# Two-block layer on one core: pass width in the plain projections, and the order of work in attention, pooling and key/value

## The chip, the cores and the metric

One core of a Trainium2 chip runs the kernel. The metric is the device time in microseconds, the median of the runs; before the change it is 3902.62 us (3 runs, 3899.95 to 3903.5). The profile is of one execution of its own, at 3903.91 us.

## The reference, cut to what matters

Two blocks follow each other on 256 tokens of width 2048, all in float32. The first: RMS norm, an input projection, a gated delta rule and a dilated attention, an output projection ("wout"), then a gated MLP with a 3-wide convolution ("up", 88 panels, and "down", 44 panels). The second also takes 256 context tokens. In short:

```
x  = x + mixed @ w_out                       # wout
up = conv3(norm(x) @ w_ffn_in); h = silu(gate) * val
x  = norm(x + h @ w_ffn_out)                 # down
h_lat, h_ctx = modulated norm of x and of ctx
q, k, v, gate = h @ w_in[...]                # q, gate: latent tokens; k, v: context too
y_na   = softmax(q k^T / 8 + bias) v         # 16 heads of 64, keys: a window and the context
y_pool = pooled mean - identity, mapped per group of channels, scaled
y_rw   = RWKV-7 scan over time, both ways, from k, v and a low-rank part ("lora")
merged = sum of gates * (branch @ w_branch);  x = x + gate * (merged @ w_out2)
```

## The kernel before, in words

A weight matrix comes in panels of 128 output channels by 2048 input channels (1 MB). SP loads panel p into one of two `ring` slots; ACT casts it to `w_hi` (fp32r, line 247), DVE subtracts it to get `w_lo` (line 253), and PE multiplies. `tick` does the cast or split of panel p+2 after panel p: the cast waits for `panel_used`, which PE raises when panel p is done, and SP loads p+2 when p is split. The activations are split in the same way. `project` (line 263) makes three passes of 256 columns for each of the 16 tiles of a panel: w_hi by x_hi, w_hi by x_lo, w_lo by x_hi, all summed in one 256-column range of PSUM bank 6 or 7. `project2` (line 278) does the same with 512 columns, latent and context tokens side by side. Matmuls of other kinds (sums over partitions, transposes, scores) have plain float32 operands.

The stages in order of time, and what they do around the change:

- wout (`add_*`, and `wout_tiles` for its first two panels). DVE adds the bank to `x` (line 1254), ACT makes `x_hi` and then casts, DVE makes `x_lo` and then splits.
- up (`up_*`). DVE multiplies the bank by the norm factor (line 1302), three convolution steps follow (1305, 1306, 1308), then the split of the panel after next, and a product or low half of the panel pair before (1290, 1294).
- down (`down_*`). 16 output tiles of 44 weight tiles each; the context tokens are normed beside it (`ctx_*`). At its end stands a chain: last bank to `x`, squares, a sum over channels on PE (line 1348), a root, a reciprocal (1471), and then for each of 16 tiles DVE (1476), ACT (1433, 1437), DVE (1479).
- attention (`na_*`). A hardware loop (Fori) of four passes on every engine, with two heads' pairs (u = 0, 1) in each. A pair has panels q, k, v, gate: q and gate by `project`, k and v by `project2`. Then come `v_rows` (1501), `scores` (1510), `turn_p` (1518) and `mix` (1527). For u = 0 these run between the panels of u = 1; for u = 1 they run after its last panel, at the end of the pass. Panel q of the first pair waits tile by tile for the chain above.
- A barrier of all engines; then GpSimd spills `x`, loads `PM` and `PWA`, and PE waits for them. Pooling (`pool_*`): a Fori loop of four, four panels each, then three small steps on PE that each wait for ACT (`u_turned`, `pooled`, `pool_y`; lines 1665 and 1672).
- A barrier; b_hi and b_lo of both branches in one piece each (2917, 2951); lora; key/value (`kv_*`): 8 pairs of panels k and v by `project2`. The sums and transposes of pair kt run after panel k of pair kt+1, those of the last pair at the end. GpSimd stores k and v to DRAM in six transfers a pair.
- A barrier; `rw_*`: 16 groups of the scan, between whose steps PE, ACT and DVE take quarters of 80 further panels (`fill_*`, each `F()` is a quarter: 4 tiles, or 12 passes of 256 columns). Five quarters precede the first group. What is left of the quarters runs at the end.
- tail, and wout2 (`last_*`), which is built like wout.

Of the kernel before, what the change touches and what calls it, by code (L numbers as in the profile page):

```python
# [152 lines left out]
def program(nc, a, out):  # L153
# [19 lines left out]
    x_hi = place("x_hi", 48, [P, KT, T], FR)  # L173
    x_lo = place("x_lo", 64, [P, KT, T], FR)
# [6 lines left out]
    def smalls(at_, n):  # L181
# [51 lines left out]
            ("na", 8, 4), ("pool", 4, 4), ("lora", 1, 1), ("kv", 2, 8), ("fill", 80, 1),  # L233
# [44 lines left out]
    def project2(pe, p, rhs, bank):  # L278
# [5 lines left out]
        for k in range(KT):  # L284
# [4 lines left out]
            last = nc.tensor.matmul(both, lo, xh, start=False, stop=k == KT - 1)  # L289
        last.then_inc(S("panel_used"), 1)  # L290
# [3 lines left out]

    bars = {}

    def barrier(eng):

        bars[id(eng)] = bars.get(id(eng), 0) + 1
        eng.drain().then_inc(S("phase_done"), 1)  # L300
        eng.wait_ge(S("phase_done"), 4 * bars[id(eng)])
# [744 lines left out]
    mx_hi = place("mx_hi", D0 + 48.5, [P, KT, T], FR)  # L1046
    mx_lo = place("mx_lo", D0 + 64.5, [P, KT, T], FR)
# [7 lines left out]
    def wout_tiles(pe, k0, k1):  # L1055
        for j in range(2):
# [5 lines left out]
            for k in range(k0, k1):  # L1062
                hi, lo = w_hi[:, s, k * P:(k + 1) * P], w_lo[:, s, k * P:(k + 1) * P]
                xh, xl = mx_hi[:, k, :], mx_lo[:, k, :]
                nc.tensor.matmul(pbank(p), hi, xh, start=k == 0, stop=False)
                nc.tensor.matmul(pbank(p), hi, xl, start=False, stop=False)
                last = nc.tensor.matmul(pbank(p), lo, xh, start=False, stop=k == KT - 1)
# [161 lines left out]
    def add_pe(pe):  # L1229
        for k in range(2, KT):  # L1230
            p = (first["wout"] + k, None, 0)
            project(pe, p, lambda t: (mx_hi[:, t, :], mx_lo[:, t, :]), pbank(p))
# [17 lines left out]
    def add_dve(dve, ch):  # L1250
        for k in range(KT):
            p = (first["wout"] + k, None, 0)
            dve.wait_ge(S("panel_used"), at(p, 3))
            nc.vector.tensor_tensor(x[:, k, :], pbank(p), x[:, k, :], ALU.add).then_inc(S("proj_read"), 1)
# [5 lines left out]
    h_hi = place("h_hi", W0 + 16, [P, FT, T], FR)  # L1260
    h_lo = place("h_lo", W0 + 60, [P, FT, T], FR)
    fraw = place("fraw", W0 + 104, [P, 2, 2, T + 2])
    fcv = place("fcv", W0 + 108.25, [P, 2, 2, T])

    def up_pe(pe):
        for k in range(2 * FT):
            p = (first["up"] + k, None, 0)
            project(pe, p, rhs_x, pbank(p))

    def up_act(act):  # L1270
# [15 lines left out]
    def up_dve(dve, ch):  # L1286
# [1810 lines left out]
```

## Time and profile before

| | |
|---|---|
| median of 3 runs | 3902.62 us |
| the profiled execution | 3903.91 us, of which the span is 3902.2 us |
| PE busy | 3585.3 us, 92% of the span |
| DVE busy | 2184.0 us, 56% |
| ACT busy | 1546.1 us, 40% |
| granted TensorE clock, mean | 0.960 of full |

The span goes from the first to the last instruction. Matmuls overlap in the record, so their durations add up to more than the time; the distance from start to start is what one of them costs.

### The profile page before, as it was taken

What the parts mean: (1) busy time and instruction counts of PE and PEld (TensorE: products, weight loads), DVE (VectorE), ACT (ScalarE), POOL (GpSimd) and SP (SyncE); (2) the same over time, 40 slices, a digit from 0 to 9 for tenths busy, and PEclk for the clock granted to TensorE, in tenths of its full rate; (3) what the DMA queues carried; (4) which work ended last, traced back from release to release, by engine and by line L of the source; (5) the groups of instructions that cost most, each with busy time, mean ns of one, the idle gap of its engine ahead of it and who ended that gap; (6) DMA issues with size and microseconds to landing.
All of it is one profiled execution on the core that took longest, in us unless ns stands there. A gap on an engine that the chain in (4) does not pass through costs nothing.

```text
span 3902.2 us, 85857 instructions
## 1 busy us (share of the span) xinstructions
PE 3585.3 (92%) x38442; PEld 3343.7 (86%) x38442; DVE 2184.0 (56%) x3247; ACT 1546.1 (40%) x2345; POOL 247.3 (6%) x306
## 2 busy tenths in 40 slices
PE   7999989999979999999978887899799999999978
PEld 7888989888879999999977776888688888888978
DVE  6666765556546777764443333345555655556554
ACT  4333333333334333334433333333444444444433
POOL 0021012000000000000000000001210111011000
PEclk9999999999989999999989998999899999999989
DMA  4534543565435555554532223324333333333354
GB/s 164 200 116 149 178 166 130 217 249 174 162 105 177 184 182 183 182 201 161 173 119 100 97 94 118 129 101 166 128 122 114 107 116 110 105 110 121 108 192 149
DMA packets 94390, 571.49 MB, mean 146 GB/s; under 512 B 12688, under 2 KB 20912, under 8 KB 32096
## 3 DMA queue, kind: packets, MB, share of 16 engines
q1 hardware_dynamic: 80496, 511.85, 37.1%
q0 software_dynamic: 13552, 54.49, 4.2%
q8 instruction: 287, 4.70, 0.5%
q14 instruction: 55, 0.45, 0.0%
HBM read 536.01 MB, written 30.28 MB: 145 GB/s over the span
## 4 chain that ended last, share of the span: by engine, by line
PE 76%; DVE 10%; ACT 6%; DMA 3%; issue 2%; POOL 1%; SPq 0%; DVEq 0%; ACTq 0%; POOLq 0%
PE banks L273 9%; PE banks L275 8%; PE banks L274 8%; PE banks L1911 3%; PE banks L966 3%; PE banks L1912 3%; PE banks L1913 3%; PE banks L967 2%; PE banks L968 2%; PE banks L1377 2%; PE banks L1379 2%; PE banks L1378 2%; PE banks L287 2%; PE banks L288 2%; PE banks L289 2%
## 5 line engine op out<-in xcount | busy, mean ns | idle before, releaser
L253 DVE TENSOR_TENSOR w_lo<-ring,w_hi 128x2048 fp32r<-128x2048 f32 x274 | 627.9, 2291 | 628.9 <-ACT w_hi L247 628.5
L247 ACT CAST w_hi<-ring 128x2048 fp32r<-128x2048 f32 x274 | 522.2, 1906 | 546.8 <-PE banks L275 388.8
L273 PE MATMUL banks<-x_hi,w_hi 128*128 128x256 f32 x1920 | 545.9, 284 | 6.8 <-DVE w_lo L253 6.5
L275 PE MATMUL banks<-x_hi,w_lo 128*128 128x256 f32 x1920 | 545.4, 284 | 0.0
L274 PE MATMUL banks<-x_lo,w_hi 128*128 128x256 f32 x1920 | 545.4, 284 | 0.0
L273 PEld LDWEIGHTS banks<-x_hi,w_hi 128*128 128x128 f32 x1920 | 370.6, 193 | 7.5 <-DVE w_lo L253 6.7
L274 PEld LDWEIGHTS banks<-x_lo,w_hi 128*128 128x128 f32 x1920 | 370.5, 193 | 0.0
L275 PEld LDWEIGHTS banks<-x_hi,w_lo 128*128 128x128 f32 x1920 | 370.5, 193 | 0.0
L1967 DVE TENSOR_TENSOR w_lo<-ring,w_hi 128x512 fp32r<-128x512 f32 x316 | 217.2, 688 | 248.4 <-ACT w_hi L1924 247.5
L966 PE MATMUL banks<-x_hi,w_hi 128*128 128x256 f32 x1152 | 349.0, 303 | 7.2 <-DVE w_lo L1033 7.2
L1911 PE MATMUL banks<-XK,w_hi 128*128 128x256 f32 x1024 | 320.3, 313 | 20.8 <-DVE w_lo L1967 20.8
L967 PE MATMUL banks<-x_lo,w_hi 128*128 128x256 f32 x1152 | 331.2, 287 | 0.0
L968 PE MATMUL banks<-x_hi,w_lo 128*128 128x256 f32 x1152 | 330.6, 287 | 0.0
L1912 PE MATMUL banks<-XK,w_hi 128*128 128x256 f32 x1024 | 293.5, 287 | 0.6 <-issue 0.6
L1913 PE MATMUL banks<-XK,w_lo 128*128 128x256 f32 x1024 | 292.8, 286 | 0.0
L1033 DVE TENSOR_TENSOR w_lo<-ring,w_hi 128x512 fp32r<-128x512 f32 x276 | 192.6, 714 | 128.2 <-ACT w_hi L1018 126.9
L966 PEld LDWEIGHTS banks<-x_hi,w_hi 128*128 128x128 f32 x1152 | 225.8, 196 | 25.3 <-issue 15.2
L1911 PEld LDWEIGHTS banks<-XK,w_hi 128*128 128x128 f32 x1024 | 199.1, 194 | 39.1 <-DVE w_lo L1967 23.1
L967 PEld LDWEIGHTS banks<-x_lo,w_hi 128*128 128x128 f32 x1152 | 226.5, 197 | 0.7 <-issue 0.5
L968 PEld LDWEIGHTS banks<-x_hi,w_lo 128*128 128x128 f32 x1152 | 225.7, 196 | 0.0
L287 PE MATMUL banks<-XK,w_hi 128*128 128x512 f32 x528 | 208.4, 395 | 1.4 <-DVEq L300 1.4
L1018 ACT CAST w_hi<-ring 128x512 fp32r<-128x512 f32 x276 | 164.3, 624 | 113.8 <-PE banks L968 65.4
(534 smaller groups left out, 8486.0 us busy)
## 6 DMA issues: line engine op xcount, KB each, us to landing
ring<-in_w_up SPq DMA_DIRECT2D x88, 1024.0 KB, 4.9
ring<-in_w_dil SPq DMA_DIRECT2D x72, 1024.0 KB, 4.9
mod_ring<-in_w_mod SPq DMA_DIRECT2D x48, 1024.0 KB, 7.6
ring<-in_w_logit SPq DMA_DIRECT2D x48, 1024.0 KB, 4.9
ring<-in_w_down SPq DMA_DIRECT2D x44, 1024.0 KB, 4.9
ring<-in_w_delta SPq DMA_DIRECT2D x32, 1024.0 KB, 4.9
ring<-in_w_out SPq DMA_DIRECT2D x32, 1024.0 KB, 4.8
ring<-in_w_na SPq DMA_DIRECT2D x32, 1024.0 KB, 4.8
```

The source lines that it names most:

```text
L247: nc.scalar.copy(w_hi[:, s, 0:w], ring[:, s, 0:w]).then_inc(S("panel_hi"), 4)
L253: nc.vector.tensor_tensor(w_lo[:, s, 0:w], ring[:, s, 0:w], w_hi[:, s, 0:w].bitcast(F32), ALU.subtract).then_inc(S("panel_split"), 1)
L273: nc.tensor.matmul(out_ap, hi, xh, start=k == 0, stop=False)
L274: nc.tensor.matmul(out_ap, hi, xl, start=False, stop=False)
L275: last = nc.tensor.matmul(out_ap, lo, xh, start=False, stop=k == tiles - 1)
L287: nc.tensor.matmul(both, hi, xh, start=k == 0, stop=False)
L966: nc.tensor.matmul(pbank(p), hi, xh, start=k == 0, stop=False)
L967: nc.tensor.matmul(pbank(p), hi, xl, start=False, stop=False)
L968: last = nc.tensor.matmul(pbank(p), lo, xh, start=False, stop=k == KT - 1)
L1911: nc.tensor.matmul(pbank(p), hi, xh, start=k == 0, stop=False)
L1912: nc.tensor.matmul(pbank(p), hi, xl, start=False, stop=False)
L1913: last = nc.tensor.matmul(pbank(p), lo, xh, start=False, stop=k == KT - 1)
```

## The change

Two edits. First, in wout, up, down and wout2 the passes are regrouped: the two activation halves lie side by side (`x_two`, `mx_two`, `h_two`, `m_two`), w_hi multiplies both in one pass of 512 columns into both halves of a PSUM bank, and w_lo multiplies the high half alone in a pass of 256 columns into the first half of the bank. The reader of the bank adds the two halves. Second, attention and pooling are written out without loops, the barriers from there to `rw_*` are gone, and the work of neighbouring stages overlaps:

- The panels of the first pair come as k, v, q, gate. `na_first` runs the context half of v and k (three passes of 256 columns a tile) before the latent half, whose tiles wait for the chain. `down_sum` of the last tile goes into it after four tiles. In the chain the gain moves from ACT to DVE, and ACT makes the high half in one activation instead of two; DVE runs two tiles behind with the low half (YB).
- Scores, turn_p and mix of each pair run between the panels of the next pair, those of the last pair between the first panels of pooling.
- Pooling's small steps run between the panels of the next group, the last group's within lora and key/value. `PM`, the spill and `PWA` are issued during attention; `PW` and its copy on GpSimd are gone. b_hi and b_lo are made in two pieces, in pooling and in the first pair of key/value.
- In key/value the sum over the squares of k runs inside panel v of the same pair; the last pair's transposes, mirrors and stores go into the start of `rw_*`, where eight quarters instead of five precede the first group. Waits on `kv_stored` stand ahead of the sigmoids (pairs 0 to 6) and of the first group (all 8), on ACT and DVE.

```
-    x_hi = place("x_hi", 48, [P, KT, T], FR)
-    x_lo = place("x_lo", 64, [P, KT, T], FR)
+    x_two = place("x_two", 48, [P, 2, KT, T], FR)
+    x_hi, x_lo = x_two[:, 0], x_two[:, 1]
...
+    def wide_tile(out_ap, hi, lo, both, first_, last_):
+        nc.tensor.matmul(out_ap, hi, both, start=first_, stop=False)
+        return nc.tensor.matmul(out_ap[:, 0, :], lo, both[:, 0, :], start=False, stop=last_)
...
+    def project_wide(pe, p, both):
+        s = p[0] % 2
+        pe.wait_ge(S("panel_split"), at(p, 3))
+        pe.wait_ge(S("proj_read"), at(p, 1))
+        for k in range(KT):
+            hi, lo = w_hi[:, s, k * P:(k + 1) * P], w_lo[:, s, k * P:(k + 1) * P]
+            last = wide_tile(wide(p), hi, lo, both[:, :, k, :], k == 0, k == KT - 1)
+        last.then_inc(S("panel_used"), 1)
...
     def up_act(act):
+                act.wait_ge(S("panel_used"), at(p, 3))
+                if i or g:
+                    act.wait_ge(S("proj_read"), at(p, 2))
+                nc.scalar.copy(fpart[:, :], wide(p)[:, 1, :]).then_inc(S("up_part"), 1)
                 tick(act, act_split, p)
...
     def up_dve(dve, ch):
-                dve.wait_ge(S("panel_used"), at(p, 3))
-                nc.vector.tensor_tensor(fraw[:, i % 2, g, 1:1 + T], pbank(p), RS[2][:, :], ALU.mult).then_inc(S("proj_read"), 1)
+                dve.wait_ge(S("up_part"), 2 * i + g + 1)
+                nc.vector.tensor_tensor(fraw[:, i % 2, g, 1:1 + T], wide(p)[:, 0, :], fpart[:, :], ALU.add).then_inc(S("proj_read"), 1)
                 dve.wait_ge(S("proj_read"), at(p, 3))
+                ch(nc.vector.tensor_tensor(fraw[:, i % 2, g, 1:1 + T], fraw[:, i % 2, g, 1:1 + T], RS[2][:, :], ALU.mult))
...
+    def na_first(pe):
+        pe.wait_ge(S("xk_ready"), KT)
+        for j in (1, 0):
+            p = na_panel(0, j)
+            pe.wait_ge(S("panel_split"), at(p, 3))
+            pe.wait_ge(S("down_read"), KT - j)
+            na_half(pe, j, 1, 0, 4)
+            if j == 1:
+                down_sum(pe, KT - 1)
+            na_half(pe, j, 1, 4, KT)
+        for j in range(2):
+            na_half(pe, j, 0, 0, KT).then_inc(S("panel_used"), 1)
+
+    def na_pe(pe):
+        na_first(pe)
+        for i in range(WT):
+            for j in range(4):
...
+                if i and j == 0:
+                    na_scores(pe, i - 1)
+                if i and j == 1:
+                    na_turn_p(pe, i - 1)
+                if i and j == 2:
+                    na_mix(pe, i - 1)
+            na_v_rows(pe, i)
+        na_scores(pe, WT - 1)
...
+    def pool_pe(pe):
+        for n in range(16):
+            p = (first["pool"] + n, None, 0)
+            g, k = divmod(n, 4)
+            project(pe, p, rhs_l, pbank(p))
+            if n == 2:
+                na_turn_p(pe, WT - 1)
+            if n == 3:
+                na_mix(pe, WT - 1)
+            if k == 3:
+                pool_turn(pe, g)
+            if k == 0 and g:
+                pool_mean(pe, g - 1)
+            if k == 1 and g:
+                pool_mix(pe, g - 1)
...
         pe.wait_ge(S("lora_ready"), 1)
+        pe.wait_ge(S("kk_root"), WT)
         wa(0)
-        for _ in range(5):
+        pe.wait_ge(S("whole_ready"), 5)
+        for _ in range(4):
+            F()
+        v_turn(pe, WT - 1)
+        for _ in range(4):
             F()
```

## Rows read from the trace of the kernel before

**Rows 1.** The page, part 1: busy us, share of the span, instructions.
```profile
PE 3585.3 (92%) x38442; PEld 3343.7 (86%) x38442; DVE 2184.0 (56%) x3247; ACT 1546.1 (40%) x2345; POOL 247.3 (6%) x306
```

**Rows 2.** Busy us by stage: window, length, engines (instructions), clock, DMA share, GB/s.
```profile
2000.80:2039.00 38.20, 17.22 (x55) 12.04 (x54) 16.98 (x37) 17.79 (x39) 0.00 (x0) 0.56 0.14 54
2039.00:2064.00 25.00, 24.87 (x108) 20.87 (x109) 8.20 (x7) 6.27 (x6) 6.75 (x6) 0.93 0.33 116
2064.00:2419.50 355.50, 309.43 (x1740) 257.24 (x1738) 146.16 (x244) 139.47 (x183) 16.46 (x18) 0.92 0.27 95
...
2433.00:2565.00 132.00, 117.36 (x848) 110.47 (x848) 40.10 (x24) 49.53 (x52) 2.45 (x4) 0.94 0.36 127
...
2767.00:2794.00 27.00, 4.04 (x10) 2.07 (x10) 11.00 (x12) 5.63 (x11) 10.65 (x17) 0.50 0.58 180
2794.00:2807.00 13.00, 11.24 (x76) 10.85 (x76) 5.33 (x12) 8.16 (x17) 3.40 (x5) 0.76 0.17 52
2807.00:3728.00 921.00, 868.44 (x17509) 800.25 (x17510) 529.76 (x921) 427.05 (x803) 88.98 (x127) 0.99 0.33 112
```

**Rows 3.** Waits of PE: who waited for whom, us in total, times, longest.
```profile
PE banks L1518 <- DVE NSc L1604: 42.3, 4, 10.6
```

**Rows 4.** Timeline of PE in up, first pass of two panels: start, us.
```profile
1299.48 0.28 PE L273 MATMUL banks<-x_hi,w_hi 128*128 128x256 f32 x1
...
1305.24 0.28 PE L273 MATMUL banks<-x_hi,w_hi 128*128 128x256 f32 x1
```

**Rows 5.** Timeline of PE in key/value, 45 passes of 512 columns apart.
```profile
2599.86 0.39 PE L289 MATMUL banks<-XK,w_lo 128*128 128x512 f32 x1
...
2610.06 0.39 PE L289 MATMUL banks<-XK,w_lo 128*128 128x512 f32 x1
```

**Rows 6.** Timeline of DVE and ACT over one panel of up.
```profile
1299.68 0.43 DVE L1302 TENSOR_TENSOR fraw<-banks,RSU 128x256 f32<-128x256 f32 x1 [1.11 <-PE banks L275]
...
1299.76 1.91 ACT L247 CAST w_hi<-ring 128x2048 fp32r<-128x2048 f32 x1 [3.53 <-PE banks L275]
...
1301.06 0.49 DVE L1308 SCALAR_TENSOR_TENSOR fcv<-fraw,small,fcv 128x256 f32<-128x256 f32 x1
...
1301.70 2.29 DVE L253 TENSOR_TENSOR w_lo<-ring,w_hi 128x2048 fp32r<-128x2048 f32 x1 [0.16 <-ACT w_hi L247]
```

**Rows 7.** Timeline of pooling: ACT copies 256 columns out of a bank.
```profile
2447.39 0.37 ACT L1682 COPY PU<-banks 128x256 f32<-128x256 f32 x1 [2.23 <-PE banks L275]
```

**Rows 8.** Chain of waits, end of down and first attention pairs: start, us, what.
```profile
2010.89 1.76 DVE RR L1471
...
2014.98 0.34 DVE yb L1476
...
2016.70 0.34 DVE yb L1476
...
2069.24 0.44 PE banks L1501 x4
2075.42 1.93 PE banks L1510 x8
...
2088.50 1.75 PE banks L1518 x16
...
2101.17 2.79 PE banks L1527 x16
```

**Rows 9.** Chain of waits over the whole span: a small step of pooling.
```profile
2494.74 2.00 PE banks L1665 x8
```

**Rows 10.** Timeline of POOL in key/value: first store of two pairs.
```profile
2723.68 0.57 POOL L1845 DMA_DIRECT2D kin_d<-KS  x1 [19.36 <-ACT KS L1785]
...
2746.88 0.57 POOL L1845 DMA_DIRECT2D kin_d<-KS  x1 [19.27 <-ACT KS L1785]
```

**Rows 11.** Timeline of ACT in key/value: the copy that waits for the stores.
```profile
2757.29 0.59 ACT L1794 COPY KS<-banks 128x512 f32<-128x512 f32 x1 [6.89 <-DMA vt_d<-VS]
```

**Rows 12.** DMA issues: queue, count, KB each, median us to landing.
```profile
ring<-in_w_up SPq DMA_DIRECT2D x88, 1024.0 KB, 4.9
...
x<-in_x SPq DMA_DIRECT2D x1, 2048.0 KB, 9.6
```

More of the change, by code:

```diff
@@ L1471, in down_dve @@
         ch(nc.vector.reciprocal(RR[:, :], RR[:, :]))
[L1472 removed]
+        for k in range(KT + YB):
             if k < KT:
@@ new lines, in na_order, with na_panel, na_v_rows, na_scores @@
+    def na_order(n):
+        return n // 4 * 4 + na_kind(n // 4, n % 4)
+    def na_panel(i, j):
+        return (first["na"] + 4 * i + j, None, 0)
+    def na_v_rows(pe, i):
+        u = i % 2
+        pe.wait_ge(S("proj_read"), at(na_panel(i, 2), 3))
+        if i:
+            pe.wait_ge(S("nvt_ready"), i)
+        for t in range(4):
+            last = nc.tensor.transpose(b4(4)[:, t, :], NAV[u][:, t * P:(t + 1) * P], C("ident"))
+        last.then_inc(S("nv_turned"), 1)
+    def na_scores(pe, i):
+        u = i % 2
+        pe.wait_ge(S("proj_read"), at(na_panel(i, 2), 3))
+        if i:
+            pe.wait_ge(S("npt_ready"), 4 * i)
+        for h in range(2):
+            for q in range(TT):
+                r = slice(64 * h, 64 * h + 64)
+                nc.tensor.matmul(banks[2 * h + q][:, :], NAQ[u][r, q * P:(q + 1) * P], NAK[u][r, :],
+                                 start=True, stop=True).then_inc(S("n_scored"), 1)
@@ new lines, in na_half @@
+    def na_half(pe, j, c, k0, k1):
+        p = na_panel(0, j)
+        s = p[0] % 2
+        for k in range(k0, k1):
+            if c == 0 and j == 0:
+                pe.wait_ge(S("xk_ready"), KT + k + 1)
+            hi, lo = w_hi[:, s, k * P:(k + 1) * P], w_lo[:, s, k * P:(k + 1) * P]
+            o = banks[6 + s][:, c * T:(c + 1) * T]
+            nc.tensor.matmul(o, hi, xk_hi(c, k), start=k == 0, stop=False)
+            nc.tensor.matmul(o, hi, xk_lo(c, k), start=False, stop=False)
+            last = nc.tensor.matmul(o, lo, xk_hi(c, k), start=False, stop=k == KT - 1)
+        return last
@@ L1568, in na_act @@
+    def na_act(act):
+        for i in range(WT):
+            u = i % 2
+            for j in range(4):
+                p, kind = na_panel(i, j), na_kind(i, j)
+                if kind == 3:
+                    nc.scalar.activation(scratch, C("ones")[:, 0:1], ACT.Silu)
                 act.wait_ge(S("panel_used"), at(p, 3))
-                if k == 3:
-                    act.wait_ge(S("na_out"), 1 + at((u, it, 2)))
+                if kind == 3:
+                    if i >= 2:
+                        act.wait_ge(S("na_out"), i - 1)
@@ L1713, in rw_params_dve, with pool_dve @@
+    def pool_dve(dve, ch):
+        for n in range(16):
+            g, k = divmod(n, 4)
+            tick(dve, dve_split, (first["pool"] + n, None, 0))
+            if n == 0:
+                na_masked(dve, ch, WT - 1, 1)
+            if n == 1:
+                na_scaled(dve, ch, WT - 1)
+            if n == 3:
+                na_put(dve, WT - 1)
+            if k == 1 and g:
+                pool_put(dve, g - 1)
+            if n == 6:
+                low_half(dve, 0)
     def rw_params_dve(dve, ch):
@@ L2525, in rw_dve @@
         a_tilde(0)
-        F()
+        for _ in range(4):
+            F()
+        dve.wait_ge(S("kv_stored"), 96 * WT)
         for g in range(NG):
@@ L2856, in _ @@
                 for k in range(per):
-                    load((first[name] + k, None, 0), a[src[name]][k, :, :])
+                    load((first[name] + k, None, 0), a[src[name]][na_order(k) if name == "na" else k, :, :])
             else:
```

585 lines of the change are left out of this document (281 added, 304 removed).

## The prediction

> **What bounds the kernel now.** I read the page first: PE is busy for 3585.3 of 3902.2 us [rows 1], so time can come from two places only, the 317 us in which PE stands still and a lower price of what it does. A table of windows by stage tells where PE stands still [rows 2]. From the end of down (2001) to the scan of the last stage (2807) there are six stretches in which it is idle, or busy at a granted clock well under 1.0: 38 us at the start of attention with clock 0.56, 355.5 us of attention with PE busy for 309 and clock 0.92, 13.5 us before pooling, 132 us of pooling with 117 busy, 27 us after key/value with 4 busy. The list of waits names the largest: at the end of each attention pass PE waits for the scaled scores, 42.3 us in four waits [rows 3]. Between 2807 and 3728 PE is busy for 868 of 921 us; that stage is dense and stays as it is.
>
> For the price of a pass I read starts in the timeline. In up the first passes of two panels lie 5.76 us apart [rows 4], which is 48 x 0.1200 us with no gap at all. In key/value 45 passes of 512 columns take 10.20 us, 0.2267 us each [rows 5]. At 2.4 GHz 256 and 512 columns take 0.1067 and 0.2133 us, so a pass costs 0.0133 us beyond its columns at either width.
>
> **Part 1, the wider pass.** A tile goes from 3 x 0.1200 = 0.3600 to 0.2267 + 0.1200 = 0.3467 us, 0.0133 less. The tiles are 256 in wout, 1408 in up, 704 in down, 256 in wout2: 2624, and 2624 x 0.0133 = 34.9 us. No row shows a pass of 512 followed by one of 256. The bounds: 0.2533 + 0.1067 at the dear end (the fixed cost stays three times), a gain of nothing, and at the cheap end 0.0266 a tile, if the weight load that a 256-column pass must cover were what costs and vanished from it too, 70 us. I take 0.0133, because the same surplus at both widths says that it belongs to the pass.
>
> The Trainium skill (TensorE: Matmul & The Clock Gate, section Back-to-back issue gap) gives the isolated gap as N/2.4 + 2.5 ns. By that a tile would save 2.5 ns and the part 6.6 us instead of 34.9. The rows have 13.3 ns, so here the rule's surplus is too small by five times; it is one of the rivals below.
>
> What the wider pass adds is in the readers of the bank, and it matters only if the supply of panels becomes late. In up, with the release of a panel as zero (1299.68 [rows 6]), today the DVE finishes its convolution at 1.86 (1301.06 + 0.48), waits for the cast, and the split ends at 4.31. The panel after next starts 5.56 later today and needs its split a weight load earlier. After the change ACT first copies half a bank, 0.37 [rows 7]; DVE adds at 0.40, 0.43 long, multiplies (0.42 by the same kind of row plus 0.04 between), then the three steps that now take 0.47 to 1.86, that is 1.39, end at 2.7; the cast (0.37 + 1.91) is done at 2.3 and no longer the later one. The split runs from 2.7 to 5.0. With panels of 16 x 0.3467 = 5.55 us the next start is at -0.20 + 5.55 = 5.35, and it needs the split at some 5.2. So the work stays hidden, with 0.2 us to spare where there was 1.1. If that cover were gone by d us, PE would lose d every second panel: 0.2 us more would cost 9 us over 88 panels. DVE work per panel is then 4.5 + 0.42 = 4.9 us of 5.55.
>
> In wout and wout2 the second add (0.45 to 0.5) lengthens the same loop to 5.6, but there PE also sums over channels between the panels (0.43 each), so the split is wanted at 6.0; nothing is lost but the first two panels of wout2 (0.4) and the longer chain at the end of each stage, 0.5 twice. In down the split has no work before it. The ring: a panel lands 4.9 us after its issue [rows 12], issue comes after the split at 5.0, the cast wants it at 11.1 + 0.4; 1.6 us to spare. Part 1 in sum: 34.9 - 1.4 = 33.5 us.
>
> **Part 2, the stretch from down to the scan.** I rebuild PE's time from its prices at full clock. A narrow panel is 5.76, a 512-column panel 48 x 0.2267 = 10.88.
>
> The start. Down ends at 2001.7; cast and split of panel 1 end at 2006.2 as now, because they need the last panel of down. PE then has the context halves of two panels, 2 x 5.76, some of it at half clock, and the sum. The chain beside it: today the reciprocal ends at 2012.65 [rows 8]. It comes 1.4 us later, since x is added in two steps (0.45) and the sum finds PE in its first four tiles at the low clock (12 passes of 0.21), so 2014.1. Today a tile takes 1.72 us (2014.98 to 2016.70 [rows 8]), DVE, ACT, ACT, DVE in a row. Two tiles behind, only DVE's own two steps count, 0.49 each and a little, 1.04 a tile. The price of an overlapped tile has no row: at least the two steps (0.98), at most 1.72, which would cost 11 us; I take 1.04, as nothing waits for itself. 16 tiles: 2030.9. The latent half of k ends with it, that of v 5.76 + 2 us (low clock at first) later, 2038.6, and q at 2044.4. Today q, k and v are done at 2064 [rows 2]. What is late next is the chain, still, and PE waits about 9 us in it.
>
> Attention from there. A pair costs 2 x 5.76 + 2 x 10.88 + 0.44 + 1.93 + 1.75 + 2.79 [rows 8] = 40.2; eight pairs less the three panels done (27.5): 294, where today 355.5 pass. The DVE's softmax (7 us masked, 2.7 scaled) starts after the split at 4.6 and ends about 14 after panel q; PE comes to turn_p 1.9 + 10.9 after it and takes 4 pieces of 0.44. That is how pairs u = 1 run today, and there turn_p follows without a wait (2088.50 [rows 8]). So 0, at most 2 us a pair.
>
> Pooling: 16 x 5.76 + 4 x (0.44 + 2.0 + 2.0) = 110 [rows 9], the third step priced as the second; today 2419.5 to 2565 = 145.5, with the transfer before it. I add 2 us for the two panels behind which DVE still has the last pair's softmax. The spill and the tables are 40 us a pair ahead.
>
> Lora and key/value: 10.88 + 8 x 23.2 = 196.5; a pair takes 23.2 today (2723.68 to 2746.88 [rows 10]) and PE is full there, so nothing is gained inside, only at both ends. Today it is 2565 to 2794, 229 us, with 27 us of sums, stores and a weight transfer behind the last panel.
>
> Sum: 2044.4 + 294 + 112 + 196.5 = 2646.9, against 2794: 147.1 us less.
>
> The start of the scan. Today 13 us pass between the first matmul at 2794 and the first group [rows 2], five quarters in them. New: the sigmoids wait for the stores of pairs 0 to 6 (4.6 us after the last panel), and mirrors and copies of the last pair, five of 0.6, stand between sigmoids and exponentials, so 13 + 5.2 = 18.2. Then ACT and DVE wait for the last stores. A pair's six transfers take 2746.88 to 2757.2 = 10.4 us [rows 10, 11]; the last begin when the copy is done at 11.2, so 21.6, and the first group is held up by about 2 more: 20.2. Queued behind that wait are ACT's copy of the first group and all of DVE's steps; PE has two matmul steps and two quarters meanwhile. The GpSimd queue could pause between issues, for which I allow 7 us. Costs 7.2 us; three quarters more are done (12 x 0.12 = 1.44 each, 4.3 us), which come back in the remainder at the end of the stage. Net 2.9 lost. The quarters' places in the groups shift by three; I put that at 0 +- 8.
>
> Part 2: 147.1 - 2.9 = 144.2 us. Together 177.7: the span goes from 3902.2 to 3724.5, the profiled time from 3903.91 to 3726. The median of the runs lies 1.3 us below the profiled one, so 3725 us.
>
> **The rivals.**
> A, new waits eat part of the second half. turn_p late by 2 us in seven pairs (14), the last stores held up by 7, the chain at 1.3 instead of 1.04 a tile (4): 25 us more, 3750. For it: softmax and split leave DVE little slack, and every reuse of a buffer that a barrier covered is now a wait. Against it: pairs u = 1 already run so without one.
> B, the supply loop in up grows past the panel. At 0.4 us past it PE loses 0.2 a panel, 18 us: 3743; at 0.8, 3760. For it: 0.2 us of cover is little. Against it: every term of the loop but the meeting of ACT and DVE is a row.
> C, the surplus does not belong to the pass but rides with the columns: a 512-column pass behind a 256-column one takes 0.240 to 0.253, a tile stays near 0.36, and part 1 brings nothing and costs its 1.4 us: 3760. Rows 4 and 5 speak against it, where the surplus is the same at both widths. The rule cited above leads to nearly this case: by it 6.6 of the 34.9 us stay, 3753.
> D, the ring. Load, cast and split of a slot form a loop of 4.9 + 1.9 + 2.3 + 0.2 = 9.3 us against two panels, 11.1. If landing rose above 6.7 us under the faster pull, the loop would set the pace, and from 10.0 on the kernel would be slower than before: at 10.4 the loop is 14.8, 7.4 us a panel instead of 5.76, 1.64 x 102 panels of up and wout = 167 us lost against the 144 of part 2, 3926 us. A transfer of 2 MB took 9.6 [rows 12], one of 1 MB 4.9; nearly excluded.
> E, the edit doesn't do what it says, PE idling under another name: 3850 or more.
>
> **How the numbers follow.** Forecast as worked out, 3710 to 3738: 0.60. A 0.20, B 0.10, C 0.04, D 0.01, E 0.02; 0.03 for a better one, if the remainder of the quarters or the down stage gives more: 3695. The range 3704 to 3760 leaves out the better end, D and E and the upper tails of A. What a measurement of this kernel can tell from no change is about 0.2%, 8 us; only D crosses it, and a bad end of E comes near, so faster 0.98, same 0.01, slower 0.01.
>
> **What would show it.** Up: panels 5.55 apart, no wait of PE for w_lo; a wait every second panel is B. A 256-column pass 0.120 after a 512-column one starts 0.227 after it; 0.253 is the dear end. L1348's chain: 1.0 to 1.1 us a tile. Attention pairs 40.2 apart, pooling groups 27.5, key/value still 23.2. First matmul of the scan about 2647 less the 32 of part 1 before it, near 2616. The clock should stand at 1.0 from the first gate panel to the scan. I am wrong if attention pairs take over 42 us, or if up takes over 495.

## The result, and the profile after

After the change the kernel takes 3724.09 us (median of 4 runs, 3721.84 to 3735.92) against 3901.28 (4 runs, 3893.04 to 3903.5): a ratio of 0.9556, 95% interval 0.9537 to 0.9574. Forecast were 3725 us. The profiled execution took 3721.84 us, its span 3720.0; the spans differ by 182.2 us, where 177.7 were forecast.

The page after the change, part 1 (busy us, share of the span, instructions), against [rows 1]:

```profile
PE 3516.5 (95%) x35914; PEld 3176.6 (85%) x35914; DVE 2236.7 (60%) x3384; ACT 1548.3 (42%) x2397; POOL 251.9 (7%) x302
```

PE is busy for 68.8 us less and idle for 113.4 us less. Both parts of the change are in this line: fewer passes, and less time in which PE stands still.

Busy time by stage after the change (window, length, then PE, weight loads, DVE, ACT, POOL; granted clock, DMA share, GB/s), which answers to [rows 2]. The windows are up, down, the start of attention, the rest of attention, pooling with lora's begin, lora and key/value, the start of the scan, the scan:

```profile
1215.00:1705.70 490.70, 489.76 (x2816) 427.84 (x2816) 412.92 (x613) 224.18 (x265) 0.00 (x0) 1.00 0.55 187
1705.70:1974.60 268.90, 267.79 (x1500) 232.27 (x1500) 130.51 (x119) 108.50 (x98) 1.06 (x2) 1.00 0.52 180
1974.60:2005.50 30.90, 26.27 (x198) 25.48 (x197) 22.70 (x43) 13.85 (x24) 2.90 (x2) 0.94 0.21 76
2005.50:2328.00 322.50, 322.50 (x1962) 275.08 (x1962) 156.52 (x249) 146.24 (x198) 29.45 (x27) 1.00 0.38 134
2328.00:2440.00 112.00, 112.00 (x786) 105.05 (x785) 38.42 (x25) 40.15 (x41) 0.00 (x0) 1.00 0.39 140
2440.00:2615.00 175.00, 175.00 (x786) 142.38 (x784) 103.52 (x122) 64.19 (x81) 26.51 (x41) 1.00 0.46 155
2615.00:2633.40 18.40, 14.17 (x122) 13.40 (x120) 11.23 (x21) 14.65 (x27) 7.44 (x11) 0.94 0.68 212
2633.40:3540.00 906.60, 859.81 (x17472) 791.85 (x17472) 522.92 (x912) 424.52 (x797) 92.08 (x131) 0.99 0.33 113
```

From 2005.5 to 2615 PE is busy in every microsecond at the clock of 1.00 (2.4 GHz), where before the stretch held pauses of 13 to 27 us and a clock of 0.92 in attention. What is left of them is in the third window, 4.4 us in which PE waits for the split of a weight panel, and in the seventh, 4.2 us before the first group of the scan.

Stage by stage, in us of the two spans:

| piece | before | after | gain | forecast |
|---|---|---|---|---|
| everything before up (wout last) | 1218.8 | 1215.0 | 3.8 | 2.9 |
| up | 507.6 | 490.7 | 16.9 | 18.7 |
| down | 275.2 | 268.8 | 6.4 | 9.4 |
| end of down to first matmul of the scan | 792.7 | 640.7 | 152.0 | 147.1 |
| scan, its start included | 995.0 | 993.2 | 1.8 | -2.9 |
| wout2 to the end | 112.9 | 111.6 | 1.3 | 2.5 |

Read by these pieces, part 1 gave 28.4 us instead of 33.5 and part 2 gave 153.8 instead of 144.2. The good total is partly luck: two errors cancel.

Two of these lines hold less than they seem to. From its first matmul to the first of up, wout takes 118.9 us before and 116.6 after, a gain of 2.4; the other 1.4 us of the first line lie ahead of wout, which starts anywhere from 1095.9 to 1103.2 us in the fourteen traces, though nothing ahead of it was changed. So part 1 is nearer to 27 us. And the scan takes 993.1 us here, while the traces below, whose scan has the same instructions, show 991.1 to 996.5, and one of them 1006.0 (run 8, where this stays unexplained). A gain of 1.8 us there is not to be told from none.

The chain of waits after the change at the start of attention (start, us, what), against [rows 8]:

```profile
1984.76 1.76 DVE RR L1481
1986.55 1.27 DVE yb L1486 x3
1987.83 0.40 DVE XK L1491
1988.22 0.40 DVE yb L1486
1988.62 0.40 DVE XK L1491
...
1998.12 0.41 DVE XK L1491
1998.57 0.38 PE banks L1567
...
2023.44 1.92 PE banks L1535 x8
...
2036.52 1.75 PE banks L1543 x16
...
2064.08 1.92 PE banks L1535 x8
```

A tile now costs 0.79 us (1987.83 to 1988.62), two DVE steps of 0.40 each. The timeline gives each of these steps a duration of 0.47 to 0.48; on one engine they start 0.40 apart.

### The profile page after: what moved, and what is told of

The parts are those of the page before. It is cut to its first block, busy times and chain, and to the rows that moved or that the text cites. A ratio compares the mean times of both kernels' runs of the same rounds, so it can differ in the third digit from the quotient of the medians.

```text
span 3720.0 us, 80273 instructions
## 1 busy us (share of the span) xinstructions
PE 3516.5 (95%) x35914; PEld 3176.6 (85%) x35914; DVE 2236.7 (60%) x3384; ACT 1548.3 (42%) x2397; POOL 251.9 (7%) x302
## 4 chain that ended last, share of the span: by engine, by line
PE 82%; DVE 9%; ACT 5%; DMA 2%; issue 2%; POOL 0%; SPq 0%; DVEq 0%; ACTq 0%; POOLq 0%
PE banks L284 16%; PE banks L285 8%; PE banks L2039 4%; PE banks L273 3%; PE banks L274 3%; PE banks L275 3%; PE banks L306 3%; PE banks L307 3%; PE banks L308 3%; PE banks L979 3%; PE banks L2040 3%; PE banks L2041 3%; PE banks L980 3%; PE banks L981 3%; PE banks L2236 2%
## 5 line engine op out<-in xcount | busy, mean ns | idle before, releaser
L284 PE MATMUL banks<-x_two,w_hi 128*128 128x512 f32 x1408 | 489.6, 394 | 0.3 <-PE banks L1065 0.3
L285 PE MATMUL banks<-x_two,w_lo 128*128 128x256 f32 x1408 | 390.6, 277 | 0.0
L979 PE MATMUL banks<-x_two,w_hi 128*128 128x256 f32 x1152 | 349.5, 303 | 7.2 <-DVE w_lo L1046 7.2
L980 PE MATMUL banks<-x_two,w_hi 128*128 128x256 f32 x1152 | 331.8, 288 | 0.0
L981 PE MATMUL banks<-x_two,w_lo 128*128 128x256 f32 x1152 | 331.4, 288 | 0.0
L284 PEld LDWEIGHTS banks<-x_two,w_hi 128*128 128x128 f32 x1408 | 264.7, 188 | 62.3 <-issue 0.7
L285 PEld LDWEIGHTS banks<-x_two,w_lo 128*128 128x128 f32 x1408 | 264.9, 188 | 0.0
L284 PE MATMUL banks<-h_two,w_hi 128*128 128x512 f32 x704 | 251.8, 402 | 2.0 <-DVE fraw L1318 0.9
L979 PEld LDWEIGHTS banks<-x_two,w_hi 128*128 128x128 f32 x1152 | 226.5, 197 | 25.1 <-issue 15.1
L980 PEld LDWEIGHTS banks<-x_two,w_hi 128*128 128x128 f32 x1152 | 227.1, 197 | 0.7 <-issue 0.5
L981 PEld LDWEIGHTS banks<-x_two,w_lo 128*128 128x128 f32 x1152 | 226.5, 197 | 0.0
L306 PE MATMUL banks<-XK,w_hi 128*128 128x512 f32 x496 | 198.9, 401 | 0.0
L2041 PEld LDWEIGHTS banks<-XK,w_lo 128*128 128x128 f32 x1024 | 196.2, 192 | 2.7 <-issue 2.7
```

What stands on the lines that cost most here:

```text
L284: nc.tensor.matmul(out_ap, hi, both, start=first_, stop=False)
L285: return nc.tensor.matmul(out_ap[:, 0, :], lo, both[:, 0, :], start=False, stop=last_)
L306: nc.tensor.matmul(both, hi, xh, start=k == 0, stop=False)
```

## The experiments

Times are medians of 4 executions in 1 to 8, one execution in 9, and medians of five in 10 to 12. Runs 10 and 11 were measured side by side, the others at other times. What a run takes "more" is counted from the 3724.09 us of the first four executions of after, the kernel after the change; run 10 shows that this lies at the lower end of what the kernel does (all nine: 3729.52), so the lengths of single stages in the traces are the better measure.

**1. The width alone (narrow_pass).** Layout, evictions and order of after, but the wide pass cut in two.

```
     if first_: one pass of 512 columns
+    else: matmul(out[:, 0], hi, both[:, 0]); matmul(out[:, 1], hi, both[:, 1])
```

> The kernel after the change, with its two-column-half layout and its two-part evictions kept, but the 512-column pass split again into two of 256 in all tiles but the first of each output tile (2488 of 2624). My theory, that the surplus of 13.3 ns belongs to the pass: tiles at 0.360 us in up and wout, so up is 1320 x 0.0133 = 17.6 us longer, wout and wout2 3.2 each, down 688 x (0.360 - 0.351) = 6.2: together 30 us, 3754. Rival, that the shorter stages come from the evictions, the clock or the order of the work and not from the width: under 10 us more, up stays near 491 us. For the down stage: if the 4 ns that a tile of down costs more than one of up come with the 512-column read of two halves 44 KB apart, down's tile is 0.360 here; if they come with anything else in that stage, it is 0.364.

3754.72 us (3749.39 to 3755.97), 30.6 more than after (25.2 more than the median of all nine; the two profiled ones differ by 27.5). Its up and down:

```profile
1217.70:1726.60 508.90, 508.00 (x4136) 503.72 (x4136) 412.93 (x613) 223.73 (x265) 0.00 (x0) 1.00 0.52 181
1726.60:2001.60 275.00, 273.89 (x2188) 269.95 (x2188) 130.42 (x119) 108.43 (x98) 1.06 (x2) 1.00 0.50 177
```

DVE and ACT do the same work in the same windows (412.9 and 224 us in up); only PE's passes differ, and up is 18.2 us longer. The width pays, and the second add and the copy cost nothing here. Down is 6.1 us longer, as expected (6.2): with narrow passes its tile is back at 0.360, so the excess of down's wide tile (0.351 instead of 0.3467) is not in the stage but in the wide pass.

**2. Part 1 alone (wide_only).** The kernel before with wide passes and their evictions.

> The kernel before with the 512-column passes and their evictions in wout, up, down and wout2 alone; attention, pooling and key/value as before, barriers and loops included. My theory, that the two parts add and that part 1 is worth the 28.5 us by which its stages got shorter: 3901 - 28 = 3873 (up 491 us, down 269). Rival, that part of the shorter stages is owed to the new schedule's placement or that the schedule's gain contains some of part 1 (the start of attention found the chain ready earlier): 3880 or more.

3877.54 us (3868.89 to 3884.67), ratio 0.9926 (0.9909 to 0.9942): 25 us less than before, where 28 were expected. So part 1 works without part 2, and the rest of the 177 us belongs to part 2. The profiled execution was one of the long ones, and its up stage says why:

```profile
1219.90:1720.00 500.10, 499.14 (x2817) 432.65 (x2817) 412.99 (x614) 223.93 (x265) 0.00 (x0) 1.00 0.52 184
```

500.1 us and not 490.7, with the same instructions and no more idle time. A tile costs 0.3533 us here throughout up, 0.3467 in the trace of after. 1408 x 0.0067 is 9.4 us.

**3. The two halves of the down activation side by side (halves_adjacent_h).**

```
-    h_two = place("h_two", W0 + 16, [P, 2, FT, T], FR)
+    h_two = place("h_two", W0 + 16, [P, FT, 2, T], FR)
```

> The kernel after the change with the two halves of the down activation side by side for each tile, so that the 512 columns of a pass are contiguous. If the distance of 44 KB between the halves is what makes a tile of down cost 0.351 us and not 0.3467: 704 x 0.0043 = 3 us less, 3721, tile 0.3467 in down. Rival, that the distance is nothing and the excess comes from the stage (its evictions, sums or DMA beside it): 3724, tile 0.351. The writes of the halves in up change by nothing in either.

3727.76 us (3720.06 to 3731.47), the mean tile of down stays at 0.351 and the stage at 268.8 us. The distance of the halves costs nothing; that idea fell. Read output tile by output tile, down shows instead that there is no 0.351: each run of tiles between two sums takes one of the two values. Timeline of PE in after, the sum over channels, then the first pass of the first and of the 43rd tile behind it, twice:

```profile
1808.50 1.03 PE L1366 MATMUL banks<-sqd,consts 128*128 128x256 f32 x4
...
1809.72 0.40 PE L284 MATMUL banks<-h_two,w_hi 128*128 128x512 f32 x1
...
1824.56 0.40 PE L284 MATMUL banks<-h_two,w_hi 128*128 128x512 f32 x1
1824.92 1.03 PE L1366 MATMUL banks<-sqd,consts 128*128 128x256 f32 x4
...
1826.13 0.40 PE L284 MATMUL banks<-h_two,w_hi 128*128 128x512 f32 x1
...
1840.69 0.40 PE L284 MATMUL banks<-h_two,w_hi 128*128 128x512 f32 x1
```

14.84 us for 42 tiles is 0.3533 each, 14.56 is 0.3467. The values in down don't look like chance either: over the last eight output tiles, six of the eleven traces with this stream show the same order of the two values (high, high, low, high, high, high, low, high), and the five others show exactly the reverse.

**4 and 5. The cover in up (up_three_copies_more, up_one_copy_more).**

```
+    for b in range(3):      # in the other kernel: range(1)
+        nc.scalar.copy(banks[b][:, 0:T], wide(p)[:, 1, :])
     nc.scalar.copy(fpart[:, :], wide(p)[:, 1, :]).then_inc(S("up_part"), 1)
```

> The kernel after the change with three more copies of half a bank on ACT before the copy that the add waits for, in each of the 88 panels of up: 3 x 0.37 = 1.11 us more in the loop from release to split. My theory (0.2 us of cover, then the loss of the excess every second panel): excess 0.9 us over a loop that spans two panels, 0.45 a panel, 40 us: 3764. If the loop had a whole panel's slack instead (the split is late only when the work of one panel fills one panel's time), DVE and ACT would still be under 5.55 us a panel and the time stays 3724.

3751.79 us (3744.3 to 3753.61), 27.7 more. Timeline of ACT and DVE over one panel of it; the three copies overlap, so the add starts 1.24 us behind the release and not 1.5:

```profile
1295.95 0.91 ACT L1294 COPY banks<-banks 128x256 f32<-128x256 f32 x3 [2.00 <-PE banks L285]
...
1296.75 0.41 ACT L1295 COPY fpart<-banks 128x256 f32<-128x256 f32 x1
...
1297.19 0.42 DVE L1320 TENSOR_TENSOR fraw<-banks,fpart 128x256 f32<-128x256 f32 x1 [1.15 <-ACT fpart L1295]
```

In after it starts 0.40 behind it, so the loop grew by 0.84; less the cover of 0.2 that is 0.64, half of it a panel, 28 us over 88. Its up is 519.0 us, 28.3 more than 490.7. DVE is busy for 413 us of it in both kernels and ACT for 296 of 519, so total work is not the limit. But the close agreement is partly luck. In up, the list of waits puts only 5.7 us on the late split (27 waits), and 20.7 us more appear as busy time of PE. Counted by the distances of starts, 22 us of the 28 lie in some 120 places where the stream is interrupted; 5.5 come from the undisturbed tiles, whose mean is 0.3510 here and 0.3467 in after. So what the late split costs by itself is about a fifth less than the rule of the prediction, half of the excess a panel, gives.

> The kernel after the change with one more copy of half a bank on ACT in front of the one that the add waits for, per panel of up. With three such copies the add began 1.24 us behind the release instead of 0.40 (0.27 to 0.30 us a copy, they overlap), and the kernel took 27 us more. My theory (cover of 0.2 us, then half the excess a panel): 0.28 more in the loop, an excess of 0.08, 0.04 a panel, 3.5 us: 3728. Rival, that the loop loses its whole excess every panel, or that ACT's or DVE's total work is what counts: 0.28 x 88 = 25 us, 3749; if the cover is wider than I think, nothing: 3724.

3731.82 us (3728.54 to 3738.29). Its up took 500.1 us at 0.3533 a tile, just what wide_only's did without the extra copy. At that pace a panel is 5.65 us long and the 0.28 fit in. So the cover is at least 0.28 us in that case, and a loss of the whole excess in every panel (25 us) is excluded; what the cover is at 0.3467 this kernel does not test.

**6 and 7. The start of attention (latent_first, four_step_chain).**

```
-    context halves of two panels, the sum in between; then latent halves
+    the sum; latent halves; then context halves                      (latent_first)

+    four steps a tile as before: DVE x*RR, ACT *GG+b, ACT cast, DVE - (four_step_chain)
```

> The kernel after the change with PE's order at the start of attention turned round: the sum and the latent halves of the first two panels first, the context halves behind them, so that nothing covers the chain of norm and scaling. My theory: the chain's tiles come 0.79 us apart from 1988 (a little earlier, since the sum is 2 us earlier), PE goes at their pace to about 1998, then the latent half of v 5.76 and the context halves 11.5, some of it at half clock: first pair ready at 2015 to 2018 instead of 2005.5, so 3724 + 11 = 3735. Rival, that PE's pace at full clock and not the cover is what made the start short: the clock has risen by the time the chain begins in either order, and the time moves by under 4 us.

> The kernel after the change with the latent scaling as it was before: four steps a tile (DVE, ACT, ACT, DVE), each tile one behind. Before, a tile took 1.72 us that way, now 0.79. My theory: 16 x 1.72 = 27.5 from 1986.5, last tile 2014.0, then the latent half of v 5.76: 2020 instead of 2005.5, 14 us more, 3738. Rival, that the chain was not on the path because PE is the bound there (PE did not wait for a tile after 1985): under 4 us.

3739.78 us (3736.13 to 3745.99) and 3742.09 us (3738.44 to 3750.22). From the last pass of down to the first pass of panel q it is 31.0 us in after, 42.2 in the first (11.2 more, expected 11) and 47.6 in the second (16.6 more, expected 14). The window of the second against the third row above:

```profile
1977.90:2025.50 47.60, 34.06 (x198) 30.60 (x197) 22.95 (x43) 20.13 (x40) 5.01 (x4) 0.75 0.14 51
```

and its timeline, PE at the latent tiles:

```profile
2003.10 0.39 PE L1570 MATMUL banks<-XK,w_hi 128*128 128x256 f32 x1 [1.10 <-DVE XK L1494]
2004.83 0.58 PE L1570 MATMUL banks<-XK,w_hi 128*128 128x256 f32 x1 [1.10 <-DVE XK L1494]
...
2009.99 0.58 PE L1570 MATMUL banks<-XK,w_hi 128*128 128x256 f32 x1 [0.71 <-DVE XK L1494]
```

with the granted clock of two stretches:

```profile
1998.00:2004.00 6.00, 2.72 (x17) 1.90 (x15) 2.50 (x7) 3.26 (x8) 0.00 (x0) 1.00 0.00 0
2008.00:2012.00 4.00, 2.31 (x7) 1.72 (x8) 2.07 (x6) 1.79 (x4) 0.00 (x0) 0.50 0.00 0
```

A tile takes 1.72 us, as before [rows 8], and the pauses cost a second time. After four tiles with pauses of 0.8 to 1.1 us in front of them, the clock falls from 1.00 to 0.50 (1.2 GHz) and stays there until 2021.5, 4.6 us behind the last late tile. The pass behind a pause goes from 0.39 to 0.58 us, the others from 0.28 to 0.41, and from the last late tile to panel q it takes 8.6 us instead of 7.0 in after. That is 1.6 of the 2.6 us beyond the expected 14. In latent_first the first late tiles come 0.79 us apart at half clock; once the clock is up, PE waits 0.17 us at each of five. So three things make the short start: the cover, the two-step tile, and a stream dense enough that the clock stays up.

**8 and 9. What sets the value of a tile (break_per_panel, break_sizes).** A small matmul into a free bank behind each panel of up.

```
     project_wide(pe, p, x_two)
+    nc.tensor.matmul(banks[5][:, 0:n], C("ones"), C("ident")[:, 0:n], start=True, stop=True)
```

> The kernel after the change with one small matmul (16 columns, fp32, into a free bank) behind each of the 88 panels of up. In the traces so far a tile of 512 + 256 columns takes either 0.3467 or 0.3533 us, and the value stays the same until the stream of passes is interrupted (in down at each sum, in up never: one value from start to end, 0.3467 in three kernels, 0.3533 in the wide passes alone). My theory, that each interruption draws the value anew: here up is a mixture by panels, mean near 0.350, 1408 x 0.0035 = 5 us more and 88 times the price of the break (0.1 to 0.2 us, 9 to 18): 3738 to 3747. Rival, that the value hangs on the stage or on addresses: all panels of up stay at 0.3467, and only the price of the breaks is added.

3757.64 us (3754.45 to 3764.39), above the 3738 to 3747 that were expected; up takes 519.3. All panels that the trace shows whole ran at 0.3533, none at 0.3467. My idea that each interruption draws the value anew fell. The interruption itself costs (519.3 - 500.1) / 88 = 0.22 us.

> The kernel after the change with a small fp32 matmul behind each panel of up whose width changes every four panels: 1, 2, 3, 4, 5, 6, 8, 12, 16, 20, 64 columns, and again. With 16 columns all 81 panels that the trace shows stayed at 0.3533 us a tile. My theory, that the break leaves the stream in one of two phases by its length: panels behind some widths run at 0.3467 and behind others at 0.3533, each width always the same. Rival 1, that any break leads to 0.3533: all panels at 0.3533. Rival 2, that it is chance at each break and the panels at 16 columns were one draw, handed on because the break restores the phase: a mixture without order by width.

One execution, 3750.28 us. Timeline of PE, first pass of the 28th to 31st panel and of the 34th to 37th (widths behind them 8, 12, 12, 12, and 16, 16, 16, 20):

```profile
1373.30 0.47 PE L284 MATMUL banks<-x_two,w_hi 128*128 128x512 f32 x1
1379.08 0.48 PE L284 MATMUL banks<-x_two,w_hi 128*128 128x512 f32 x1
1384.95 0.47 PE L284 MATMUL banks<-x_two,w_hi 128*128 128x512 f32 x1
1390.72 0.48 PE L284 MATMUL banks<-x_two,w_hi 128*128 128x512 f32 x1
...
1408.24 0.47 PE L284 MATMUL banks<-x_two,w_hi 128*128 128x512 f32 x1
1414.02 0.48 PE L284 MATMUL banks<-x_two,w_hi 128*128 128x512 f32 x1
1419.89 0.48 PE L284 MATMUL banks<-x_two,w_hi 128*128 128x512 f32 x1
1425.76 0.48 PE L284 MATMUL banks<-x_two,w_hi 128*128 128x512 f32 x1
```

Panels alternate, 5.78 and 5.87 us, up to the 34th, whatever the width; from the 35th on all 54 take 5.87, at width 1 again too. None of the three theories fits: the value looks like a state that the stream carries on and that an interruption can turn over or leave, and the width of the small matmul alone doesn't choose it. What does is open.

**10. The same kernel again (after_again).**

> The kernel after the change once more, to see how far one kernel's executions spread. In eight traces the up stage ran at 0.3467 us a tile all through (491 us), at 0.3533 (500 us), or switched between them behind interruptions. If the value is settled anew at the start of each execution's up stage, the times fall around two centres some 9 us apart, 3722 and 3732, smeared by a few us from down, and the median lies between 3722 and 3732. Rival, that it belongs to the compiled kernel: all times within 3 us of each other.

Five times from 3725.48 to 3737.67, median 3733.56. The profiled one, at 3733.56, has this row for up, against 490.70 in the first trace of the same program:

```profile
1215.40:1715.40 500.00, 499.09 (x2816) 432.48 (x2816) 413.11 (x613) 223.80 (x265) 0.00 (x0) 1.00 0.54 184
```

So the program does not fix the value. Whether it is settled anew in each execution, or by something else that differed between the two measurements, two traces can't tell. Of the eight traces whose up has no break or wait of its own, four show 0.3467 and four 0.3533. All nine times of this kernel have their median at 3729.52; the 3724.09 of the first four, and my 3725, lie at the lower end. Two clean centres are not to be seen in nine times, and up is not the only thing that spreads them: of the 11.8 us between the two profiled executions 9.3 are in up and 3.4 in the scan. The prediction called itself wrong if up took over 495 us; one of the two traces of its own kernel does.

**11. More wide passes (wide_more).** The q and gate panels of attention and all of pooling, 512 tiles, read out as in up.

> A candidate for a better kernel: the 512-column pass also in the q and gate panels of attention and all panels of pooling (32 panels of 16 tiles), read out as in up by a copy of one half on ACT and an add on DVE; the gates' Silu follows behind the add. My theory: 512 x 0.0133 = 6.8 us if those tiles run at 0.3467, 3.4 at 0.3533, no new wait of PE, since ACT and DVE have a third of the stage free: 3 to 7 us less than the kernel after the change in the same job. Rival, that the third interruption between panels (v_rows, scores, turns) leaves little of it or that the longer chain from q to scores makes PE wait: no gain, or up to 8 us more.

3724.93 us (3720.36 to 3732.3) against 3733.56 measured beside it, 8.6 less, but how much of that is the luck of up can't be told from five times each (its trace had 490.7 there, that of after_again 500.0). From the end of down to the scan it is 637.3 us against 640.7 and 640.5: 3.3 us, the lower end of what was expected, since about three quarters of these tiles, in short runs, show 0.3533.

**12. Passes grouped by width (grouped_wide_more).**

```
     for k in range(KT):
         nc.tensor.matmul(wide(p), hi, both[:, :, k, :], start=k == 0, stop=False)
-        nc.tensor.matmul(wide(p)[:, 0, :], lo, both[:, 0, k, :], start=False, stop=k == KT - 1)
+    for k in range(KT):
+        nc.tensor.matmul(wide(p)[:, 0, :], lo, both[:, 0, k, :], start=False, stop=k == KT - 1)
```

> The kernel wide_more (the 512-column pass in 32 more panels), and in up, down, wout2, attention and pooling the passes of a panel grouped: first the 16 of 512 columns with the high weights, then the 16 of 256 with the low ones, instead of 512, 256, 512, 256. Streams of one width show one value in every trace (0.120 at 256 in up of the kernel before, 0.2267 at 512 in key/value); two values occur only where the widths alternate. My theory, that the 6.7 ns are paid at alternations in one phase: grouped, a tile costs 0.2267 + 0.120 = 0.3467 in every panel whatever the execution, up 491, down 266 instead of 269, attention and pooling another 3 us less than in wide_more: all executions near or under wide_more's best, 3714 to 3720, within 5 us of each other. Rival 1, that the step to another width has a price whenever it comes and the phase only moves it: 2 changes a panel instead of 32, the same or less. Rival 2, that the second value belongs to the execution and not to the alternation: up is 0.3533 on average in half of the executions and their spread stays 16 us.

3717.9 us, five times from 3715.38 to 3720.68, ratio to before 0.9529 (0.9516 to 0.9542). The spread over five is 5.3 us, where wide_more has 11.9 and after_again 12.2 over five each. Timeline of PE over two panels of up:

```profile
1300.22 3.82 PE L294 MATMUL banks<-x_two,w_hi 128*128 128x512 f32 x16
1303.88 2.08 PE L297 MATMUL banks<-x_two,w_lo 128*128 128x256 f32 x16
1305.79 3.82 PE L294 MATMUL banks<-x_two,w_hi 128*128 128x512 f32 x16
1309.44 2.08 PE L297 MATMUL banks<-x_two,w_lo 128*128 128x256 f32 x16
```

A panel takes 5.57 us, 16 x 0.3467 and 0.02. Behind the first two, all panels of up start 5.56 or 5.57 apart. Up is 492.2 us, down 267.8, from the end of down to the scan 635.8. The times are those of the theory, and rival 2, that the spread stays 16 us, fell in five executions; that up never takes a second value here rests on one trace. Rival 1, a price for each change of width, is not excluded, but at two changes a panel it is at most the 0.02 us above. The kernel is 183 us faster than before and 11.6 faster than the median of after's nine; against wide_more, which makes the same passes in the other order, it is 7.0.

## Why the prediction was right, and where it was not

**The price of a wide tile** (0.0133 us saved) was right for one of two cases. The prediction added a tile from a step of 0.2267 behind the wide pass and one of 0.1200 behind the narrow one. Where a tile takes 0.3467, the traces show its sum but not its terms: 0.2317 and 0.1150 on average, over some 1300 tiles in each of four traces. Where it takes 0.3533 (four traces), they are 0.2364 and 0.1169. Up in the profiled execution had the first value, so its term came out near the forecast (16.9 of 18.7). Of the 1.8 us that are missing, 1.5 are the first five tiles of up: the granted clock of its first 3 us was 0.50 after and 1.00 before; why is open. Down had both values by turns: 0.351 on average, 704 x 0.0043 = 3.0 us, just the shortfall of 6.4 against 9.4. This is the term of part 1 that was mis-sized. Which value up gets was luck: in the second trace of the same kernel all of up had the higher one, and the term was worth half. That is a weak form of rival C, which I gave 0.04: a surplus that comes with the alternation takes half of the saving of a tile, not all of it. Neither stream of one width that the prediction read shows it, and no alternation was there to read [rows 4, 5].

The Trainium skill (TensorE: Matmul & The Clock Gate, section Back-to-back issue gap) gives N/2.4 + 2.5 ns for an isolated matmul. Run 1 shows that it can't be used for this stream: the width of 1320 tiles was worth 18.2 us in up, where that rule would give 1320 x 2.5 ns = 3.3. The section says itself that the formula leaves out the weight load.

**The cover in up** was right. The split ended 4.92 us behind the release (forecast 5.0), and PE never waited for it. Run 4 gave 28.3 us for 0.84 us more, of which 22 are interruptions; half of the excess a panel says 28. That the cover is just 0.2 us was not measured. Rival B didn't occur.

**The start of attention**: 31.0 us, forecast 36.9. The failed step is "only DVE's own two steps count, 0.49 each and a little, 1.04 a tile". The durations of the timeline include a part that overlaps with the next instruction; start to start a step is 0.40 us, a tile 0.79, and 16 x 0.25 = 4 us come from that. "PE waits about 9 us in it" became 0.2: with the faster chain PE reaches the last tile together with it, at 1998.57. Runs 6 and 7 show what the forecast could only assume: the cover is worth 11 us, and the two-step tile 17.

**Attention, pooling, key/value.** Two scores 39.8 us apart on average (2023.38 to 2302.05 in seven pairs; forecast 40.2), pooling groups 26.9 (27.5), and no wait at turn_p, which was rival A's first item. Key/value pairs take 23.6 us on average (first stores from 2466.43 to 2607.90, six pairs) where 23.2 were forecast; the pair that the prediction read was one of the shortest, five of them before the change average 23.3 (2653.92 to 2770.51). The prediction did not count that the sum now stands between the passes of panel v, one more interruption a pair. Run 8 prices one at 0.22, which would explain the rest; it was not tested. In sum it is 609.7 us from panel q to the scan against 608.3. No run takes the second part to pieces here: what the written-out loops, the missing barriers and the new order are worth one by one is not known.

**The start of the scan** took 18.2 us from its first matmul (2615.24) to the first group (2633.47). That is the 18.2 of the sum without the hold, but the path is another one, so the number is luck. The hold of 2 us by the last stores was not there: they landed and the values of the first group went out at 2633.80, but PE's first steps did not need them. Instead the first group waited for its keys. The chain of waits, with the two transfers of values behind it from the timeline of POOL:

```profile
2609.20 2.08 POOL vt_d L1979 x3
2611.28 6.86 issue
2618.15 2.54 DMA vt_d<-VS
...
2621.00 2.14 POOL KIN L2806 x3
2623.14 4.07 DMA KIN<-kin_d
2627.30 0.70 DVE BT__179 L2566
...
2633.47 1.13 PE banks L2269 x32
```

```profile
2626.83 2.78 POOL L1979 DMA_DIRECT2D vt_d<-VS  x4
2633.80 2.85 POOL L2815 DMA_DIRECT2D Vtok<-vt_d  x4 [4.20 <-DMA vt_d<-VS]
```

The queue of GpSimd paused for 6.9 us ahead of the last store of pair 6, and it does so at the same place in the five other traces that I read for it. The forecast had allowed for up to 7, but behind the last stores of all, in rival A. The sigmoids waited for that store until 2620.72, 1.7 us after ACT was ready, and so did the loads of the keys, for which DVE then waited 3.3 us more. So the pause is on the path, and the first group would start earlier without it; by how much no run shows.

The rest of the scan was 4.7 us shorter than forecast when the hold is counted. That is within the 0 +- 8 that I had put on the places of the quarters, and within what traces with the same scan differ by.

**The chances.** The forecast's own case held in both parts. Of A only the pause of the queue occurred; B, D and E did not. The range from 3704 to 3760 covers all nine times, and so does 3710 to 3738, though I had not foreseen what spreads them. That the median of the first four lay within 1 us of the forecast is luck: part 1 fell short, part 2 gave more, and up had the lower of its two values in the profiled execution.

## What to carry to other kernels

Where passes of two widths follow each other, group them: the same 32 passes of a panel took 492 us in up, where by turns they took 491 or 500, and the spread over five executions fell from 12 us to 5. Price a chain on one engine by the distance of starts, not by the durations that the timeline gives (0.40 against 0.48 here). Price a producer loop over two buffers against two panels: here about half of what it overshot was lost per panel, and nothing below its slack. And when a forecast number comes true, look whether the path to it did: the 18.2 us at the start of the scan did by another one.

## What the runs showed of the hardware

- A stream of fp32r passes of 512 and 256 columns by turns takes 0.3467 or 0.3533 us a pair; of the 6.7 ns between them 4.7 are in the step behind the wide pass. The value held for 490 us on end, differed between two traces of one program, and changed only where something interrupted the stream. The streams of 256 columns (0.120 in up before) and of 512 (0.2267 in key/value) and the grouped panels (5.57) showed one value.
- A small fp32 matmul between passes cost 0.22 us (run 8), and the distance of panels was the same 5.87 us at every width from 1 to 64 columns in run 9.
- With no pause longer than 1.1 us, one in every 1.72, the granted clock fell from 1.00 to 0.50 in run 7, and passes went from 0.28 to 0.41 us: a chain that feeds PE slowly is paid twice.
- Four copies of 256 columns on ACT took 1.2 us together (run 4), where one alone took 0.37 [rows 7].
